# Fused two-block network, one core: stage handovers by token half, scales at evictions, rows by DMA

## The reference

```python
f = swiglu(rmsnorm(h, nw[0]), gate, up, down);  h = h + 0.5 * rmsnorm(f, nw[1])
m = mixer(rmsnorm(h, nw[2]), ...);              h = h + rmsnorm(m, nw[3])
f = swiglu(rmsnorm(h, nw[4]), gate, up, down);  h = h + 0.5 * rmsnorm(f, nw[5])

def rmsnorm(x, w): return x * rsqrt(mean(x * x, -1) + 1e-6) * w
def swiglu(x, w_gate, w_up, w_down): return (silu(x @ w_gate) * (x @ w_up)) @ w_down
```

## Time and profile before

| what | value |
|---|---|
| median of three runs | 3381.14 us |
| span of the profiled execution | 3381.2 us |
| mean granted TensorE clock | 0.910 |
| PE, DVE, ACT, POOL busy | 86, 67, 47, 17% of the span |
| chain that ended last | PE 75%, DVE 18%, ACT 4%, issue 2% |
| DMA | 661.33 MB, mean 196 GB/s |

### The profile page before, as it was taken

The page is one execution under the profiler, slowest core; times in us unless marked ns, Lnnn a source line. Parts: engine busy times, 40 slices in busy tenths (PEclk is TensorE's granted clock), DMA queues, the critical chain, the costliest instruction groups (busy, mean ns, idle before and its releaser), DMA issues.

```text
span 3381.2 us, 35753 instructions
## 1 busy us (share of the span) xinstructions
PE 2905.1 (86%) x12969; PEld 2351.0 (70%) x12969; DVE 2264.2 (67%) x2463; ACT 1594.1 (47%) x1914; POOL 587.7 (17%) x293
## 2 busy tenths in 40 slices
PE   6979556896998966899786899789999999999997
PEld 5868355685787853688664688667777777777775
DVE  4553634787854656554535688468888888888887
ACT  3434211443443433443324344237767677767675
POOL 0000000799910000000220599400000000000000
PEclk9989567898997977999897999879999999999999
DMA  6534001566752510464210688328889898898984
GB/s 229 187 126 161 1 0 38 184 234 217 261 187 89 172 40 8 154 199 162 100 50 7 213 293 283 109 85 325 319 319 338 298 341 319 322 329 308 334 329 155
DMA packets 278531, 661.33 MB, mean 196 GB/s; under 512 B 13727, under 2 KB 22777, under 8 KB 278425
## 3 DMA queue, kind: packets, MB, share of 16 engines
q1 hardware_dynamic: 264840, 607.81, 50.5%
q0 software_dynamic: 13584, 52.07, 4.7%
HBM read 658.79 MB, written 1.05 MB: 195 GB/s over the span
## 4 chain that ended last, share of the span: by engine, by line
PE 75%; DVE 18%; ACT 4%; issue 2%; SPq 0%; DVEq 0%; DMA 0%; ACTq 0%
PE ps L1614 21%; PE ps L1616 21%; PE ps L1615 20%; DVE w_lo L996 6%; PE ps L1779 2%; ACT w_hi L642 1%; PE ps L1684 1%; PE ps L2035 1%; DVE xt L1024 1%; DVE act_lo L1031 1%; DVE xt L1049 1%; DVE xt L1260 1%; PE ps L1911 1%; PE ps L1949 1%; PE ps L1661 1%
## 5 line engine op out<-in xcount | busy, mean ns | idle before, releaser
L996 DVE TENSOR_TENSOR w_lo<-w_raw,w_hi 128x1024 fp32r<-128x1024 f32 (+1 forms) x1156 | 1513.9, 1348 | 456.9 <-ACT w_hi L642 440.9
L642 ACT ACTIVATE w_hi<-w_raw 128x1024 fp32r<-128x1024 f32 (+1 forms) x1156 | 1190.7, 1053 | 770.1 <-PE ps L1616 765.8
L1614 PE MATMUL ps<-w_hi,act_hi 128*128 128x512 f32 (+1 forms) x3424 | 1353.6, 395 | 140.9 <-DVE w_lo L996 123.9
L1616 PE MATMUL ps<-w_lo,act_hi 128*128 128x512 f32 (+1 forms) x3424 | 1335.6, 390 | 0.0
L1615 PE MATMUL ps<-w_hi,act_lo 128*128 128x512 f32 (+1 forms) x3424 | 1334.6, 390 | 0.0
L1614 PEld LDWEIGHTS ps<-w_hi,act_hi 128*128 128x128 f32 x3424 | 656.3, 192 | 298.5 <-DVE w_lo L996 103.5
L1616 PEld LDWEIGHTS ps<-w_lo,act_hi 128*128 128x128 f32 x3424 | 655.4, 191 | 134.6
L1615 PEld LDWEIGHTS ps<-w_hi,act_lo 128*128 128x128 f32 x3424 | 656.8, 192 | 126.7 <-issue 0.2
L557 POOL TENSOR_TENSOR scr<-scr 128x1024 f32<-128x1024 f32 x98 | 291.2, 2971 | 8.2
L690 ACT ACTIVATE act_hi<-xt 128x512 fp32r<-128x512 f32 (+1 forms) x87 | 66.5, 765 | 334.2 <-DVE xt L1049 334.2
L555 POOL TENSOR_SCALAR scr<-scr,small 128x1024 f32<-128x1024 f32 x98 | 198.1, 2022 | 6.4
(11 more groups left out here) (377 smaller groups left out, 1745.3 us busy)
## 6 DMA issues: line engine op xcount, KB each, us to landing
w_raw<-in_moe_w SPq DMA_DIRECT2D x336, 1024.0 KB, 6.1
scr<-in_ada_w POOLq DMA_DIRECT2D x48, 1024.0 KB, 6.0
w_raw<-in_ffn_w_gate SPq DMA_DIRECT2D x44, 1024.0 KB, 5.2
w_raw<-in_ffn_w_up SPq DMA_DIRECT2D x44, 1024.0 KB, 5.1
w_raw<-in_ffn_w_down SPq DMA_DIRECT2D x44, 1024.0 KB, 4.9
w_raw<-in_ff_w SPq DMA_DIRECT2D x42, 1024.0 KB, 5.2
w_raw<-in_odd_w_in SPq DMA_DIRECT2D x20, 1024.0 KB, 5.0
w_raw<-in_even_w_in SPq DMA_DIRECT2D x14, 1024.0 KB, 5.1
```

Of the source, the lines that this page charges most:

```text
L642: act.activation(w_hi[:, g % SPLITS, 0:c * width], w_raw[:, s % RING, o:o + c * width], ACT.Copy).then_inc(hi_done, 1)
L996: dve.tensor_tensor(w_lo[:, g % SPLITS, 0:c * width], w_raw[:, s % RING, o:o + c * width], w_hi[:, g % SPLITS, 0:c * width].bitcast(F32), ...
L1614: pe.matmul(out_ap, hi, whi, start=start, stop=False)
L1616: return pe.matmul(out_ap, hi, wlo, start=False, stop=stop)
```

## The change

- **Handover.** `boundary` takes the place of `residual` and `norm` at five places, `start` that of the first norm, and a new `residual` with the same beginning stands before attention. The last four down granules (`tail`) run for token half 0 first, then for half 1. Half 0 is squared, rooted (epsilon as the bias, 1/1024 as the scale), multiplied and added to `h` while half 1 is still multiplied. PE transposes `h` itself, not `xn`; the pre-norm column is applied when ACT and DVE split out of PSUM (`h_split`, four pieces of 128 columns a call). The first four granules of the next stage (`lead`) are multiplied for half 0, then for half 1.
- **1/rms** of the pre-norm (`rn`) is applied at the evictions of the gate, up and projection products: per token half as `scale=` of ACT's Silu and Copy, and in DVE's product.
- **The post-norm row** comes by a broadcast DMA into `wbc` (`post_row`), issued by SP ahead of a given slot's load, after a wait that the old row was read. `row_diag`, `row_broadcast` and `row_copy` stay for the second block.
- **Gated blocks**, all of them: ACT and DVE split the hidden block straight from banks 6 and 7 (no copy to `xt`); PE's second `up` waits for `hlo_done` in place of `hid_x`; DVE keeps the last `w_lo` of a step for after its product; in the last step, one down granule (two in the expert loop) stands ahead of the last transposes and the rest behind.
- `split_banks` splits the transposed output of the even and odd mixers straight from banks 4 to 7, and `down` there waits for pairs of chunks.
- `mod_columns` moves into the gated block (`closing`). POOL's waits count `hh_done` in place of `h_ready`, for the same handovers.

```diff
+        def post_row(l, j, sem=None, count=0):
+            row_loads[len(slots) + RING if slots else 0] = (t["norm_w"][l, j], sem, count)
...
             for s in range(n_slots):
+                if s in row_loads:
+                    row, freed, count = row_loads[s]
+                    if count:
+                        sp.wait_ge(freed, count)
+                    sp.dma_start(wbc[:], row.partition_broadcast(P)).then_inc(wbc_in, 16)
                 load(s)
...
         def _(act):
+            def h_split(tb, half, col, bank):
+                act.wait_ge(ht_done, n(ht_done))
+                for i in range(4):
+                    c = 4 * half + i
+                    ins = act.activation(act_hi[:, c, tb * P:(tb + 1) * P], ps[:, bank + i // 2, (i % 2) * P:(i % 2 + 1) * P], ACT.Copy,
+                                         scale=col[:, c:c + 1])
+                    if i % 2:
+                        ins.then_inc(nhi_done, 1)
+            def post_sums(tb):
+                if tb == 0:
+                    act.wait_ge(br_done, n(br_done))
+                else:
+                    act.wait_ge(gran_used, tail_end[0])
+                act.activation(xn[:, tb, :], banks(2 * tb, 2), ACT.Square, accum_out=ssq[:, tb:tb + 1]).then_inc(act_sum, 1)
+                act.wait_ge(act_sum, n(act_sum))
+                act.activation(rt[:, tb:tb + 1], ssq[:, tb:tb + 1], ACT.Sqrt, bias=epsc[:, 0:1], scale=1.0 / DM).then_inc(bt_done, 1)
+            def boundary(col, late):
+                tail_end[0] = gp[0]
+                act.activation(epsc[:, 1:2], epsc[:, 0:1], ACT.Sqrt)
+                post_sums(0)
+                hi(2)
+                h_split(0, 0, col, 6)
+                post_sums(1)
+                h_split(0, 1, col, late)
+                hi(2)
+                h_split(1, 0, col, 6)
+                h_split(1, 1, col, 2)
+                pre_sums()
+                act.activation(epsc[:, 1:2], epsc[:, 0:1], ACT.Silu)
...
                 def hidden(i):
-                    act.wait_ge(hid_x, n(hid_x))
-                    src = xt[:, 1024 * (i % 2):1024 * (i % 2) + c * tbs * P].rearrange("p (c n) -> p c n", c=c)
+                    act.wait_ge(hid_t, n(hid_t))
+                    src = banks(6, tbs)[:, 0:c * tbs * P].rearrange("p (c n) -> p c n", c=c)
...
         def _(dve):
+            def add_post(tb, factor):
+                dve.wait_ge(bt_done, n(bt_done))
+                link(dve.reciprocal(rstd[:, tb:tb + 1], rt[:, tb:tb + 1]))
+                for k in range(2):
+                    cols = slice(k * BANK, (k + 1) * BANK)
+                    dve.scalar_tensor_tensor(xn[:, tb, cols], ps[:, 2 * tb + k, :], rstd[:, tb:tb + 1], wbc[:, cols],
+                                             ALU.mult, ALU.mult).then_inc(dve_link, 1)
+                for k in range(2):
+                    cols = slice(k * BANK, (k + 1) * BANK)
+                    dve.wait_ge(dve_link, n(dve_link))
+                    dve.scalar_tensor_tensor(h[:, tb, cols], xn[:, tb, cols], factor, h[:, tb, cols],
+                                             ALU.mult, ALU.add).then_inc(hh_done, 1)
+            def boundary(factor, col, late):
+                dve.wait_ge(wbc_in, n(wbc_in, 16))
+                add_post(0, factor)
+                lo(1)
+                h_split(0, 0, col, 6)
+                lo(1)
+                add_post(1, factor)
+                h_split(0, 1, col, late)
+                lo(2)
+                h_split(1, 0, col, 6)
+                h_split(1, 1, col, 2)
+                next_rstd()
...
                     if i:
-                        split(2 if s[i - 1][1] == BANK else 1)
+                        lo(grans(s[i - 1][1]) - 1)
                     dve.wait_ge(silu_done, n(silu_done))
...
+                    if i:
+                        lo(1)
...
         def _(pe):
+            def lead(bank, first=False):
+                for tb in range(TB):
+                    for k in range(4):
+                        g = gp[0] + k
+                        c, width, _ = granule(g // 2, g % 2)
+                        pe.wait_ge(lo_done, g + 1)
+                        pe.wait_ge(nlo_done, n(nlo_done))
                         for i in range(c):
+                            ins = three(ps[:, bank + tb, 0:width], 2 * k + i, slice(tb * P, tb * P + P), g, i * width, width,
+                                        k == 0 and i == 0, k == 3 and i == 1)
+                        if tb:
+                            ins.then_inc(gran_used, 1)
+                        if tb == 0 and k == 1:
+                            h_transposes(1, 0, 6, first)
+                            h_transposes(1, 1, 2, first)
+                gp[0] += 4
+            def tail(chunks, free=None):
+                for tb in range(TB):
+                    for k, chunk in enumerate(chunks):
+                        g = gp[0] + k
+                        pe.wait_ge(lo_done, g + 1)
+                        for nh in range(2):
+                            ins = three(ps[:, 2 * tb + nh, :], chunk, slice(tb * P, tb * P + P), g, nh * BANK, BANK, False, k == 3)
+                        if tb:
+                            ins.then_inc(gran_used, 1)
+                        elif k == 3:
+                            ins.then_inc(br_done, 1)
+                        if tb and k >= 2 and free is not None:
+                            h_transposes(0, k - 2, free if k == 3 else 6)
+                gp[0] += 4
...
                     if i:
-                        pe.wait_ge(hid_x, n(hid_x))
+                        pe.wait_ge(hlo_done, n(hlo_done))
                     up(per, [(0, b, 6 + k) for k, b in enumerate(blocks)])
                     if beside:
                         beside(i)
-                    if i:
-                        pe.wait_ge(hlo_done, n(hlo_done))
-                        down(2 if s[i - 1][1] == BANK else 1, 8 + 4 * ((i - 1) % 2), i == 1, False, tbs)
-                    hidden(i)
+                    if i < last:
+                        if i:
+                            down(chunks(i - 1), i == 1, tbs=tbs)
+                        hidden(i)
...
+                early = 1 if tbs == TB else 2
+                rest = chunks(last - 1) + chunks(last)
+                down(rest[0:early], tbs=tbs)
+                hidden(last)
+                if scaled:
+                    if closing:
+                        closing()
+                    down(rest[early:-4])
+                    pe.wait_ge(hlo_done, n(hlo_done))
+                    return rest[-4:]
```

633 lines of the change are left out of this document (368 added, 265 removed).

## The result

The changed kernel takes 3189.6 us (median of four runs, 3182.8 to 3197.6) where the kernel before takes 3382.1: ratio 0.943, 95% interval 0.941 to 0.945. The forecast was 3217, range 3180 to 3264. Its profiled execution spans 3187.4 us, 193.8 less than that of before, where the sum had 164.6.

What follows compares the result with a forecast made beforehand. The prediction took TensorE, busy 86% of the span, as the bound, losing time at handovers and expert-block stalls. Gains of 98.2 plus 66.4, together 164.6 us, taken from 3381.2 gave 3217 us, range 3180 to 3264.

Steps and rivals of the forecast that it cites:

- Start, 4.5: Kernel start: DVE no longer waits for rstd, weights are split first, lead ends near 42.7 instead of 47; gain 4.5 us.
- First handover, 18.8: First stage handover: time not spent on weight products falls from 27.4 to 8.6 us, gain 18.8 us.
- Between the feed-forwards, 22: Handover between the two feed-forwards, with POOL busy: loss falls from 41.9 to 20 us, gain 22 us.
- 4.6 more by POOL and 6.8 that stay: Between the feed-forwards: slower w_lo and adds lengthen DVE's chain 4.6 us; 6.8 stay for first hidden block and POOL stalls.
- Before odd, 9.3: Handover before the odd mixer: column sums stay on PE's path, loss falls from 44.4 to 35.1 us, gain 9.3 us.
- Odd, 15.6: Odd mixer's down projection: its start saves 4.5 of 17.4 us, its handover falls from 20.3 to 9.2; gain 15.6 us.
- Expert block, 8.45: Expert loop: stalls within and at the end of a block shrink by 8.45 us, 66.4 us over eight blocks.
- (a): Handovers more bound by DVE's queue, with clock low for the whole lead and longer small pieces: 3264 us; chance 0.13.
- (b): Expert loop held elsewhere, by DMA engines or DVE, so half its gain goes: 3250 us; chance 0.11.
- (c): All holes close at handovers and blocks: clock stays up, small hops vanish, 36 us less, 3181 us; chance 0.10.
- (d): Gated blocks slower: PE waits for DVE's late hidden-block subtraction once its 2.6 us margin is gone: 3389 us; chance 0.02.
- (e): Handovers: ACT's order holds the next stage's w_hi behind post_sums and both halves; 80 of 98 us stay, 3297; chance 0.04.

Runs made afterwards that it cites:

- the second profile: Changed kernel run once more, nothing edited: 3193.9 us, ratio 0.944; its profiled even mixer took 9.0 us more than in the first execution.
- the ten runs: Ten profiled runs with the changed kernel's even mixer code: 245.4 to 255.1 us from the 407th to the 424th product, mean 251.6.
- the run with the pause: Version with the shorter start, POOL's modulation sums also pausing until the handover between the joined feed-forwards is over: 3165.7 us, ratio 0.937.
- the run that took it away: Changed kernel with DVE's subtraction of a hidden block moved behind the four w_lo of the step's second product: 3563.3 us, ratio 1.052.

## Why the prediction was right, and where its sum was off

The mechanism, the sign and the order of the three largest terms were right, and the time lies in the range, 27 us under the forecast. Part of the distance is luck: 6 to 9 us of the profiled gain are the clock in the even mixer. The rest is errors of both signs. By the steps of the sum:

- **Start, 4.5, was 1.6.** Two terms failed: "the row costs 1.3", and a table load put at nothing. First weights land at 23.8 instead of 21.6 us, and ACT's first table load of 1.28, which stood in idle time before, now stands behind them, ahead of the first split. The version with both out of the way, and 13 small loads with them, gains 12.3. The load in the kernel before:

```profile
0.72 1.28 ACT L663 ACT_TABLE_LOAD   x1 [0.72 <-PEq L2122]
```

- **First handover, 18.8, was 21.2.** DVE's queue ran nearly as reckoned: first quarter of h at T0 + 3.8, third granule at T0 + 12.6 (reckoned 13.5). A piece took 0.28 us on DVE, not 0.33, and 0.286 on ACT, as in the earlier trace rows. Of the 2.4 us too much, 0.9 is this queue and 0.4 the clock: it had 2.0 us after the hole, where here a hole of 1.51 us is followed by eight products at half clock, 1.6 us, and in other executions by nothing (the same stretch took 34.7 and 33.1 us). The rest is within the 0.8 us for small hops and the 0.4 for hidden transposes, which were not read apart. The Trainium skill ("VectorE: DVE Perf Modes", The TRN2 errata) argued against small pieces; their fixed part is real (256 columns cost 0.33 and 0.37 where two pieces cost 0.57), but the run with larger pieces moved the third granule by half a microsecond.
- **Even mixer, 0, was 9.5.** No step spoke of it, because nothing in it was changed. Most of it is where the clock fell in that one execution, as the second profile shows. With the mean mixer of the ten runs the profile's gain would be 187.6.
- **Between the feed-forwards, 22, was 28.2.** The step "4.6 more by POOL and 6.8 that stay" put the longer w_lo and adds on PE's path in full. Together they are 11.4 us over the first handover; measured are 6.8. The w_lo did take 2.0 to 2.2 us, the adds 1.15 to 1.6; but the run with the pause shows at most 4 us of it in the handover. That the lead's products and half 1 cover the rest is argued, not shown.
- **Before odd, 9.3, was 14.2.** The column sums cost 25.1 us (read from the products around them; reckoned 25.5): right. The handover around them lost 5 instead of 9.6, for the reasons of the first one.
- **Odd, 15.6, was 12.4.** The handover gained 12.8 (reckoned 11.1). The start of the down projection gained nothing in its window and 2.0 with what precedes it, not 4.5: PE still waits 3.67 us there, for w_lo and not for the eviction that I had saved:

```profile
1255.08 0.79 PE L1798 MATMUL ps<-w_hi,act_hi 128*128 128x512 f32 x1 [3.67 <-DVE w_lo L1114]
```

- **Ends of the feed-forwards**, 9.5 and 6.0, were 8.1 and 8.6.
- **Expert block, 8.45, was 9.0**, period 127.6. Undone, the copy costs 5.3 in most blocks (its stalls were reckoned at 4.55) and the end 3.3 on average (reckoned 3.9). Of the two new stalls only one came, 0.49 where 0.45 and 1.05 were reckoned; the gathering's rest is 0.77 (0.7 reckoned):

```profile
2365.26 0.50 PE L1798 MATMUL ps<-w_hi,act_hi 128*128 128x512 f32 x1 [0.77 <-DVE w_lo L1114]
2400.12 0.50 PE L1798 MATMUL ps<-w_hi,act_hi 128*128 128x512 f32 x1 [0.49 <-DVE w_lo L1114]
```

Of the rivals, (a) is out: the clock in the handovers is 0.93 to 1.00 where it stands alone. (b) is out: DMA runs at 0.95 and 347 GB/s, as reckoned, and no product waits for it. (c), all holes close, was the nearest in time, though the waits of 0.47 and 1.51 are still there. (d) was real in kind and did not happen: the margin held, and the run that took it away shows that I had priced it too low. I had 1 us for each us of wait where the clock makes it 1.3 to 1.5, and counted the loop's 48 steps only; 26 steps of the dense stages have the same wait. (e) is out by the timeline above.

## What to carry to other kernels

Put a stage handover on a timeline from the moment when half of its input is done, one row for each engine's queue, and each handover's term comes out within 1.4 to 6.2 us; do the same for the first 30 us, table loads and small DMA issues included. Before crediting a change with a gain, look whether it lies where the change is: an unchanged stage in which TensorE takes turns with other engines can differ by 9 us between two executions of the same kernel. Where TensorE works in short turns, products that nobody reads, sized to end before the wait does and written to a bank that is free, can be worth as much as a reworked handover: 18 to 20 us here for two calls. Try it place by place: in the attention heads it gave nothing.

## What the hardware showed that was not expected

- The granted clock fell and rose within loops whose waits are 0.69 and 1.47 us; with these waits filled it stayed at full speed in eight of ten levels (sixteen products 2.05 us instead of 3.7). In the attention heads it stayed at half with the waits filled down to 0.28 us.
- A TensorE wait of 3.1 to 4.3 us cost 4.9 us on average in a block, the rest being products at half clock behind it; one of 1.5 us cost 0 to 1.6 more than itself.
- Beside a busy POOL, DVE's fp32 operations with both inputs in SBUF took 1.65 times as long (w_lo 1.22 to 2.0, add 0.69 to 1.15), one that reads PSUM 0.745 and 0.747.
- SyncE issues a small DMA in 0.25 to 0.54 us (one took 1.04), so 13 loads that nobody needs yet and the row, issued first, put the request for the first weights from 7.3 to 14.6 us.
- ACT's first instruction carries a table load of 1.28 us even if it is a copy. In the changed kernel the load ran only when the wait for the first weights was over, at 23.84 us; in the kernel before it ran at 0.72, far ahead of the data at 19.04 that its instruction waited for. What decides this was not looked at.
